# A decoder step on one core: half of the late key pages on another queue, seven value pages earlier, the result stored in four parts

## The reference

```python
q, k, v, u = project_in(x, l, attn_norm, w_in, q_norm, k_norm)      # 2048 -> 5120 columns
k_past = cache_k[l][page_table].reshape(db, past_len, 2 * N_HEADS, HEAD_DIM)
v_past = cache_v[l][page_table].reshape(db, past_len, N_HEADS, 2 * HEAD_DIM)
o = diff_attn_core(q, k_all, v_all, q_pos, k_pos, lam)              # softmax(1) - lam * softmax(2), times v
c, cs = conformer_conv(u, state_conv[l], dw_w[l], dw_b[l], conv_ln_g[l], conv_ln_b[l])
x = x + jnp.concatenate([oa, c_out], axis=-1) @ w_out[l]
h = rms_norm(x, mlp_norm[l]) @ w_up[l]                              # 2048 -> 8192
y = x + jnp.square(jax.nn.relu(h)) @ w_down[l]                      # 8192 -> 2048
```

## Time and profile before

| | us |
|---|---|
| runs of before | 1622.68, 1622.88, 1639.64 (median 1622.88) |
| the profiled execution | 1632.08 |
| its span, first to last instruction | 1630.4 |
| busy: TensorE, VectorE, ScalarE, GpSimd | 1514.5, 975.2, 593.8, 419.7 |
| value pages, 120 from SP into `v_page` | 512 KB each, median 7.6 from issue to landing |
| key quarters, 512 from POOL | 128 KB each, median 6.6 |
| chain that ended last | TensorE 72%, issue 10%, VectorE 7%, DMA 5%, GpSimd 3% |

### The profile page before, as it was taken

How to read it: one execution, slowest core, us unless ns; L and a number is a source line. 1 busy time by engine, 2 the same in 40 slices (tenths; PEclk the granted TensorE clock), 3 DMA queues, 4 the chain that set the end, 5 groups by cost and what they waited for, 6 DMA issues and landing times.

```text
span 1630.4 us, 31305 instructions
## 1 busy us (share of the span) xinstructions
PE 1514.5 (93%) x11203; PEld 1348.6 (83%) x11203; DVE 975.2 (60%) x1469; ACT 593.8 (36%) x929; POOL 419.7 (26%) x656
## 2 busy tenths in 40 slices
PE   5999898797877868899999999999999999999998
PEld 5988766565654433599999999999999999999998
DVE  3689857998998775353645544455444554445444
ACT  4433312122222332443544433443334433344432
POOL 4597656765787653000000000000000000000000
PEclk9999998998997977799999999999999999999999
DMA  7746799999999776834555545555455545555444
GB/s 201 215 144 185 234 321 333 353 341 327 342 305 349 252 236 221 289 118 154 155 158 165 168 167 162 164 165 166 167 166 162 164 165 167 167 163 163 165 166 148
DMA packets 163845, 340.50 MB, mean 209 GB/s; under 512 B 33915, under 2 KB 33971, under 8 KB 163168
## 3 DMA queue, kind: packets, MB, share of 16 engines
q1 hardware_dynamic: 120592, 267.29, 51.1%
q0 software_dynamic: 43168, 72.15, 14.5%
HBM read 334.00 MB, written 5.96 MB: 209 GB/s over the span
## 4 chain that ended last, share of the span: by engine, by line
PE 72%; issue 10%; DVE 7%; DMA 5%; POOL 3%; POOLq 2%; ACT 1%; SPq 0%; ACTq 0%
PE acc L691 21%; PE acc L693 21%; PE acc L692 21%; DMA k_page<-in_cache_k 3%; PE aux L777 2%; DVE k_page L1536 2%; POOL k_page L579 1%; PE aux L842 1%; POOLq L574 1%; DVE w_lo L1454 1%; DMA raw<-in_w_in 1%; PE acc L945 1%; PE aux L801 1%; POOLq L579 1%; PE acc L965 1%
## 5 line engine op out<-in xcount | busy, mean ns | idle before, releaser
L1454 DVE TENSOR_TENSOR w_lo<-raw,w_hi 128x1024 fp32r<-128x1024 f32 x368 | 451.5, 1229 | 410.2 <-ACT w_hi L1124 409.3
L691 PE MATMUL acc<-a_hi,w_hi 128*128 128x288 f32 (+1 forms) x1920 | 591.8, 308 | 35.2 <-DVE w_lo L1454 26.4
L1124 ACT CAST w_hi<-raw 128x1024 fp32r<-128x1024 f32 x368 | 384.9, 1049 | 586.5 <-DMA raw<-in_w_down 255.4
L693 PE MATMUL acc<-a_hi,w_lo 128*128 128x288 f32 (+1 forms) x1920 | 578.4, 301 | 0.0
L692 PE MATMUL acc<-a_lo,w_hi 128*128 128x288 f32 (+1 forms) x1920 | 578.2, 301 | 0.0
L691 PEld LDWEIGHTS acc<-a_hi,w_hi 128*128 128x128 f32 x1920 | 367.6, 191 | 72.5 <-DVE w_lo L1454 36.5
L579 POOL DMA_DIRECT2D k_page<-in_cache_k x512 | 332.1, 649 | 204.5 <-issue 89.3
L692 PEld LDWEIGHTS acc<-a_lo,w_hi 128*128 128x128 f32 x1920 | 368.3, 192 | 0.5
L693 PEld LDWEIGHTS acc<-a_hi,w_lo 128*128 128x128 f32 x1920 | 368.4, 192 | 0.0
L693 PE MATMUL acc<-h_hi,w_lo 128*128 128x288 f32 x1024 | 302.2, 295 | 0.0
L692 PE MATMUL acc<-h_lo,w_hi 128*128 128x288 f32 x1024 | 301.5, 294 | 0.0
(11 more groups left out here) (224 smaller groups left out, 892.6 us busy)
## 6 DMA issues: line engine op xcount, KB each, us to landing
k_page<-in_cache_k POOLq DMA_DIRECT2D x512, 128.0 KB, 6.6
raw<-in_w_up SPq DMA_DIRECT2D x128, 512.0 KB, 3.7
raw<-in_w_down SPq DMA_DIRECT2D x128, 512.0 KB, 3.6
v_page<-in_cache_v SPq DMA_DIRECT2D x120, 512.0 KB, 7.6
raw<-in_w_in SPq DMA_DIRECT2D x80, 512.0 KB, 6.0
raw<-in_w_out SPq DMA_DIRECT2D x32, 512.0 KB, 3.7
k_page<-in_cache_v SPq DMA_DIRECT2D x8, 512.0 KB, 5.5
x_nat<-in_x_prompt SPq DMA_DIRECT2D x3, 1024.0 KB, 8.9
```

Source lines behind the costliest of these rows:

```text
L691: mm(out, wh, ah, start=(kt == 0), stop=False)
L693: last = mm(out, wl, ah, start=False, stop=(kt == KT - 1))
L1124: nc.scalar.copy(w_hi[:, j % RAW], raw[:, j % RAW]).then_inc(hi_ok, 1)
L1454: v.tensor_tensor(w_lo[:, j % RAW], raw[:, j % RAW], w_hi[:, j % RAW].bitcast(F32), ALU.subtract)\
```

## The change

Three parts.

1. The first seven value pages of sequence 0 are issued earlier: pages 0 to 5 by `load_first` after the odd chunks of the third visit and the first two odd chunks of the fourth, page 6 in the last but one step of the fifth. Pages 0 to 3 go to the four slots, pages 4 to 6 to places that are free then (two in `z`, one in `tmp`), so the later pages' slots are shifted by three (`before_values`). `body(0)` issues from page 7 on. SP's loop over three visits is written out.
2. From page 104 on (page 8 of sequence 6; `SPLIT`) POOL issues quarters 0 and 2 of a key page and SP quarters 1 and 3 (`half_keys`), for four pages at a time, ahead of the value page of every fourth step (`key_group`). VectorE waits for both semaphores.
3. The result's columns of a down visit are turned in the next visit, after its k-tiles 4, 6 and 8 (`turn_columns`), copied by ScalarE and VectorE between their chunks (`keep_y`) and stored by SP after the next visit's loads; only the last group is left to the end, its transposes tile by tile as the adds finish.

The diff, cut to its core:

```diff
+EXTRA = 3
+Y_SLOTS = {4: 0, 6: 1, 8: 2}
+SPLIT = N_PAGES * (PAIR_V + 1) + KS
+        first_values = [z_late[:, 0:D_ATTN], z_late[:, D_ATTN:2 * D_ATTN], flat_tmp[:, 0:D_ATTN]]
+        def before_values(s, i):
+            n = N_PAGES * s + i
+            return n if n < VR else n - EXTRA
...
             def load_values(s, i):
-                slot = i % VR
-                sp.wait_ge(pv_mm, N_PAGES * s + i + 1)
+                slot = before_values(1, i) % VR
+                if isinstance(s, int) and s == 0 and i < 2 * VR + EXTRA:
+                    sp.wait_ge(pv_mm, i - EXTRA + 1)
+                else:
+                    sp.wait_ge(pv_mm, N_PAGES * s + i + 1)
...
+            def half_keys(s, j):
+                r = sp.value_load(pages_sb[0:1, ds(N_PAGES * s + j, 1)], min_val=0, max_val=n_phys - 1)
+                sp.wait_ge(sc_mm, NG * s + j // SG - 1)
+                for b in (1, 3):
+                    sp.dma_start(key_quarter(j % KS, b), key_rows(r, b)).then_inc(kh_in[j % KS], 16)
+            def key_group(i):
+                if i % SG == 0 and SPLIT + i < N_PAGES * N_SEQ:
+                    for j in range(SPLIT + i, SPLIT + i + SG):
+                        half_keys(j // N_PAGES, j % N_PAGES)
...
-            with sp.Fori(1, ATT_FIRST) as n:
+            for j in range(NC):
+                load_w(1, j, w_src(1, j))
+            sp.wait_ge(pages_in, 16)
+            sp.wait_ge(sq_x, 3)
+            for n in range(2, ATT_FIRST):
                 for j in range(NC):
                     load_w(n, j, w_src(n, j))
+                    i = (NC * (n - 2) + j) // 2
+                    if j % 2 and i < VR + 2:
+                        load_first(i)
...
                 for j in range(N_PAGES):
-                    if j + 2 < N_PAGES:
-                        if vs is not None:
+                    if keys:
+                        keys(j)
+                    if vs is None:
+                        if j == N_PAGES - 2:
+                            sp.wait_ge(nrm_v, 1 + 2 * MT * NORM_VISITS)
+                            load_first(VR + 2)
+                    elif j + 2 < N_PAGES:
+                        if not isinstance(vs, int) or vs or j + 2 >= VR + EXTRA:
                             load_values(vs, j + 2)
...
-            with sp.Fori(PAIR_V, N_SEQ - 2) as s:
-                body(s)
+            body(PAIR_V, keys=key_group)
             for i in range(2, N_PAGES):
+                key_group(N_PAGES + i - 2)
                 load_values(N_SEQ - 2, i)
...
-                for b in (0, 2, 1, 3):
+                for b in (0, 2, 1, 3) if whole else (0, 2):
                     pool.dma_start(key_quarter(slot, b), key_rows(r, b)).then_inc(k_in[slot], 16)
...
+            def turn_columns(g):
+                def between(kt):
+                    if g >= 0 and kt in Y_SLOTS:
+                        pe.wait_ge(acc_free, MT + MT * (n0 + UP_N + g + 1))
+                        for m in range(MT):
+                            turn_y(g, Y_SLOTS[kt], m)
+                return between
+            for d in range(DOWN_N):
+                down(n0 + UP_N + d, N_QTR - 1, turn_columns(d - 1))
+            g = DOWN_N - 1
+            for m in range(MT):
+                pe.wait_ge(acc_free, MT + MT * (n0 + UP_N + g) + m + 1)
+                for i in range(3):
+                    turn_y(g, i, m)
```

More of the change, by code:

```diff
@@ L241, in build_step @@
         k_in = [sem(f"k_in{r}") for r in range(KS)]
+        kh_in = [sem(f"kh_in{r}") for r in range(KS)]
         v_in = [sem(f"v_in{r}") for r in range(VR)]
+        vx_in = [sem(f"vx_in{r}") for r in range(EXTRA)]
         vk_in = [sem(f"vk_in{r}") for r in range(VR)]
@@ L570, in _, with load_keys @@
                 pool.dma_start(conv_sample[0, s, 0:TAPS - 1 - DEC, :], st[s, DEC:TAPS - 1, :]).then_inc(kc_out, 16)
-            def load_keys(s, j, used=True):
+            def load_keys(s, j, used=True, whole=True):
                 r = pool.value_load(pages_sb[0:1, ds(N_PAGES * s + j, 1)], min_val=0, max_val=n_phys - 1)
@@ L1087, in down @@
                     products(n, kt, h_hi, h_lo, 0, T_OUT)
+                    if between:
+                        between(kt)
             out_visit(OUT_V0 + 1, 0, first=True)
@@ L1430, in _, with keep_y @@
                 up(n0 + u, N_QTR - 1, u)
-            with act.Fori(0, DOWN_N - 1) as d:
-                visit(n0 + UP_N + d)
-            visit(n0 + UP_N + DOWN_N - 1, last=True)
-            for b in range(0, 12, 2):
-                g, i = b // 3, b % 3
-                n = P if i < 2 else N_SMP
-                dst = y_nat[:, i, VC * g:VC * (g + 1)] if i < 2 else y_smp[:, VC * g:VC * (g + 1)]
-                act.wait_ge(y_mm, b + 1)
-                nc.scalar.copy(dst, aux[0:n, b % 4, :]).then_inc(y_a, 1)
+            def keep_y(g, i):
+                b, n = 3 * g + i, P if i < 2 else N_SMP
+                if g >= 0 and i in range(3) and b % 2 == 0:
+                    act.wait_ge(y_mm, b + 1)
+                    nc.scalar.copy(y_rows(g, i), aux[0:n, b % 4, :]).then_inc(y_a, 1)
+            for d in range(DOWN_N):
+                visit(n0 + UP_N + d, last=d == DOWN_N - 1, between=lambda j: keep_y(d - 1, j - 4))
+            for i in range(3):
+                keep_y(DOWN_N - 1, i)
         @block.vector
@@ L1975, in invert_x2, with down @@
                     dve.wait_ge(x2_v, 1)
-            def down(n, d, last=False):
-                visit(n, lambda: add_x(n, MT * d), last=last)
+            def down(n, d, last=False, between=None):
+                visit(n, lambda: add_x(n, MT * d), last=last, between=between)
             up(MLP_V0, 0, 0, invert_x2)
@@ L1992, in _, with keep_y @@
                 up(n0 + u, N_QTR - 1, u)
-            with dve.Fori(0, DOWN_N - 1) as d:
-                down(n0 + UP_N + d, d)
-            down(n0 + UP_N + DOWN_N - 1, DOWN_N - 1, last=True)
-            for b in range(1, 12, 2):
-                g, i = b // 3, b % 3
-                n = P if i < 2 else N_SMP
-                dst = y_nat[:, i, VC * g:VC * (g + 1)] if i < 2 else y_smp[:, VC * g:VC * (g + 1)]
-                dve.wait_ge(y_mm, b + 1)
-                v.tensor_copy(dst, aux[0:n, b % 4, :]).then_inc(y_d, 1)
+            def keep_y(g, i):
+                b, n = 3 * g + i, P if i < 2 else N_SMP
+                if g >= 0 and i in range(3) and b % 2:
+                    dve.wait_ge(y_mm, b + 1)
+                    v.tensor_copy(y_rows(g, i), aux[0:n, b % 4, :]).then_inc(y_d, 1)
+            for d in range(DOWN_N):
+                down(n0 + UP_N + d, d, last=d == DOWN_N - 1, between=lambda j: keep_y(d - 1, j - 4))
+            for i in range(3):
+                keep_y(DOWN_N - 1, i)
 _INS = ["x_prompt", "x_sample", "cache_k", "cache_v", "state_conv", "page_table", "meta_tokens", "attn_norm",
```

84 lines of the change are left out of this document (56 added, 28 removed).

## The result

| | before | after |
|---|---|---|
| median, us | 1624.18 | 1650.49 |
| profiled execution, its span | 1632.08, 1630.4 | 1650.3, 1648.6 |
| ratio to before | | 1.014, 95% interval 1.0111 to 1.017 |
| forecast | | 1620.9, range 1610 to 1632 |

The ratio is not that of the medians (1.016), because one of the four runs of before took 1639.64.

What follows compares the result with a forecast made beforehand. TensorE bounds 690 to 1620 us, DMA engines are full in the sixth visit, and engines hand over small pieces in 524 to 660. -3.1 + 0.3 + 2.1 - 2.3 + 1.0 = -2.0 from 1622.88 gives 1620.9 us, range 1610 to 1632.

Steps and rivals of the forecast that it cites:

- the price of SP's half page: SP's issue of two key quarters: say 1.5 us, 6 a group of four; other bound 2.1 and 8.3 from POOL's issue.
- the fifteenth page: Sequence 5's value page behind the last stop: issued about 592.3 instead of 588.55, 3.7 us late, net +2.1.
- The second and third stops: Groups of half key pages ahead of sequence 5's value pages: a step or more to spare, so no cost.
- the first or second stop: Sign of error: a value page waited for at these groups of half key pages; the first was covered by 2 us.
- swallowed by VectorE's wait: After the last stop, VectorE's 1.57 us wait for ScalarE's exponentials absorbs that much: 3.7 - 1.6 = +2.1.
- The gain of the split: Last key group, first page issued at 620.18: last page lands some 5 us earlier, removing TensorE idle time, -2.3 us.
- Rival D: SP's queue: dearer issues and key bytes delay value pages, +8.9 us, 1631.8; decides once the fifteenth page is over 1.6 late; chance 0.12.
- Rivals A and B: Early values: A, every moved byte comes back, -10.8 for -3.1, chance 0.14; B, values hidden anyway, 0 for -3.1, chance 0.14.
- The forecast -3.1: Sixth visit: two of sequence 0's early value pages leave the crowded DMA stretch, -3.1 us, bounds nothing and 10.8.
- The +0.3 in the third and fourth visits: Six early value pages there can delay weight chunks behind them: +0.3 us, bounds 0 and 3.
- Rival C: TensorE's clock at 640 to 660 us stays at 2.4 GHz once idle pieces go: -8, 1612.9 us; chance 0.10.
- The stores: Last three visits and end: nine transpose groups cost +5.0 between products, end 4.0 shorter; +1.0 us, bounds 0 and +3.2.

Runs made afterwards that it cites:

- e13: Changed kernel with POOL issuing all four key quarters; SP only reads page numbers and waits for the scores at the half pages' places, issuing nothing. Ratio 0.9974.
- e5: Changed kernel with SP's two transfers of a key page carrying the same bytes as 32 plain rows of 4096 bytes. Ratio 1.0007.
- e9: Changed kernel with SP issuing one quarter of a key page in place of two, and POOL three. Ratio 1.0141.
- e12: Changed kernel with POOL issuing all four quarters and SP issuing same-pattern transfers with 16-byte pieces to memory that nothing reads. Ratio 1.015.
- e1: Changed kernel with the split of the key pages undone; early values and visit-by-visit stores stay. Ratio 0.9966 to the kernel before.
- e2: The kernel before with the split of the key pages alone. Ratio 1.0119.
- e3: The kernel before with the seven early value pages alone. Ratio 0.9976.
- e8: Changed kernel with 20 extra SP transfers of 128 KB in five patterns in the last quarter, to price an issue by pattern. One run, 1647.86 us.
- e15: Changed kernel, split in groups of four kept, with 16 in place of 8 in the key pages' rows. Ratio 1.051 to the kernel before.
- e16: Early values and stores without the split, with 16 in place of 8 in the key pages' rows. Ratio 1.0457 to the kernel before.

## Why the prediction was wrong

**The step that failed** is the price of SP's half page, "say 1.5, and 6 us for a group of four". It measured 3.0 to 3.6, and 12.15. I took it from a value page's row, adding one issue of the same price, and took POOL's 0.66 as the upper bound. The first row has another pattern than a key quarter and the second another engine, and on SP the price hangs on the pattern: 0.33 us for whole rows, 0.78 for this, for the same bytes, and 0.78 in place of 0.27 for the load behind it, which neither row shows. The bound of 8.3 us a group was no bound. Price against harm, for page 14 of sequence 5:

| kernel | first key issue to value page's issue, us | TensorE waits, us | ratio |
|---|---|---|---|
| e13, no issues | | 0 | 0.9974 |
| e5, plain rows | 6.38 | 3.70 | 1.0007 |
| e9, one quarter | 8.28 | 6.39 | 1.0141 |
| after | 12.15 | 8.12 | 1.014 |
| e12, no bytes | 12.13 | 8.88 | 1.015 |

Only e9 falls out of order: a cheaper group, and the whole loss.

With about the price that I forecast, e5, TensorE waits 3.70 us for page 14 and 0.85 for page 15, 4.5 together; the prediction had worked out 3.7 (its 592.3 for the fifteenth page is 0.4 more than its own 590.8 and pitch of 1.09 give). So for this stop the working behind the price held: fed with 12.15 in place of 6 it gives 3.7 + 6.1 = 9.8, and 8.12 + 1.29 = 9.4 came. That e5 as a whole came near the forecast time is luck: its stretch is 7.4 us longer than in e1, not 2.1, and what follows makes most of that good.

**"The second and third stops have a step or more to spare"**: at 6 us a group nearly so (2.1 us for page 6, at the second stop, in e5), at 12 not: 3.43 us for page 6. The first stop of sequence 6, which the sum put at nothing, cost 4.8 for its page 2. The text had said that a value page waited for at the first or second stop would show it wrong; page 6 is at the second, and in e2, e9 and e12 page 2, at the first, is waited for too (2.1, 1.3 and 3.5 us).

**What was left out of the sum** is the clock. The prediction let 1.6 us of a late page be swallowed by VectorE's wait; at most 0.8 were, for from page 15's first product to the next scores it took 5.0 us before and 4.2 after. In the stretch the waits for values are 12.8 us, and TensorE's busy time is 3.0 more than in e1 for the same matmuls (40.93 against 37.88), at a granted clock of 0.80 against 0.90: 15.8 us, of which other waits gave back 1.5, for a loss of 14.3. The idle pieces are paid again in slower products behind them: the eight of page 14 take 1.05 us, those of page 15 in the earlier trace rows 0.62. The first output visit shows the same by itself: a gap of 3.8 us, then 1.2 GHz, 6.2 us in all, though there not by the split alone. Only the chance of 0.05 for slower by over 1%, which "needs D and a slower clock behind it", names both together, and that is what came.

**The gain of the split** is there, but does not pay. The key page of the earlier trace rows is off the chain, and VectorE's wait for a key page, 1.66 in the earlier trace rows and 4.1 in e1 between 520 and 692 us, is gone. In e5 the rest of the body, from page 15 of sequence 5 to the first output visit, is 5.7 us shorter than in e1 (83.1 against 88.8, one profile each), more than the 2.3 forecast; in the changed kernel it is 0.9 longer (89.7), with page 2 of sequence 6 late. A cheaper issue would thus have made the split worth nothing or a little less (1.0007 against 0.9966). The rule of the Trainium skill cited in the prediction, that a second issuing engine saves only the sequencer's time, comes to about the same (DMA: Bandwidth & Descriptors, "Issuing engines are not separate DMA queues"). It adds that this time is usually small relative to the transfer; here the time of the issues was enough for all of the loss.

**Rival D** named the mechanism and its turning point, a fifteenth page over 1.6 us late; page 14 was waited for 8.1 us and page 15 for another 1.3. Its sum (1631.8) was too low: it used POOL's price and left out the second stop and the clock. The 3.1 us that it put on key bytes ahead of the value page in SP's queue aren't needed, as e12 shows.

**Rivals A and B**: the sixth visit is 1.9 us shorter (2.2 in e1), VectorE's waits there went from 21.4 to

```profile
DVE k_page L1633 <- DMA k_page<-in_cache_k: 19.6, 9, 3.7
```

and up to the tenth visit after, e1 and e3 gain 4.4, 7.8 and 3.8 in all. Single profiles scatter as much: of the kernels with 8 in the key pages' rows, the eleven with the early values start the tenth visit at 450.9 to 457.5, the four without at 456.2 to 458.7. The means differ by 3.5, 2.0 of it in the sixth visit. The forecast -3.1 was right in kind, and neither A nor B; that some of the gain came past the sixth visit, I had excluded. The +0.3 in the third and fourth visits didn't show (and eight chunks in 33 us are one every fourth microsecond, not every third).

**Rival C** did not come: the 0.76 in 640 to 660 us belongs to earlier work, since the body runs some 13 us later, and the last sixteen score products take 3.61 us as they took 3.64 in the earlier trace rows. In e5 they take 1.92, which is part of its shorter rest. After the change, then in e5:

```profile
657.12 3.61 PE L842 MATMUL aux<-k_page,q_cur 128*32 128x512 f32 x16 [0.91 <-DVE k_page L1633]
```

```profile
641.98 1.92 PE L844 MATMUL aux<-k_page,q_cur 128*32 128x512 f32 x16 [0.91 <-DVE k_page L1635]
```

**The stores** were forecast at +1.0 and measured -0.7 in the profiles. A visit with three groups of transposes is 1.3 us longer, 0.44 a group of four where I took 0.55. From the end of the last add to the end of the last issue it is 4.3 us shorter (forecast 4.0): 1643.67 to 1646.33, where before it was 1620.81 to 1627.73. DVE's and SP's timelines:

```profile
1642.02 1.65 DVE L2010 TENSOR_TENSOR xT<-xT,acc 128x288 f32<-128x288 f32 x4 [5.01 <-PE acc L758]
...
1645.88 0.45 SPq L569 DMA_DIRECT2D out<-y_smp  x1
```

## What to carry to other kernels

A DMA that is handed to another engine's queue brings the time of its issue with it, and that time is set by the pattern, not the bytes: before moving one, find a row of the same pattern on that engine, or measure it with a few transfers that nothing waits for, and multiply by all that stands ahead of the next urgent instruction. Moving work to a queue that is idle on average helps only if the queue has the time where the work lands: 4.1 us of issues a step can't go under steps of 3.3 us, grouped or spread. And a wait can cost more than its length where TensorE's clock falls behind it: 12.8 us of waits came with 3.0 us of slower products here.

## What the runs showed of the hardware that was not expected

- An issue on SP takes 0.33 us for plain rows, 0.57 for several pieces on each of 32 partitions, 0.72 to 0.79 (up to 0.96 at most) when the source's first stride counts 8, and then the next load of a register takes 0.78 in place of 0.27. Pieces of 16 bytes cost the same as pieces of 1024 (e8, e12).
- With 16 for 8 in that stride the issue falls to 0.61 and the load to 0.27 (e15). On POOL the same edit cuts the issue from 0.65 to 0.55 us and makes the kernel 4.6% slower, while value pages from SP land in 15.2 us in place of 7.6 (e16).
- What stays open: why a visit is met at the one or the other clock from kernel to kernel, how the loss of e9 divides between slower landing, the clock and the rest of the body, and why e16 is slower.
